# Sparse attention loop: compressed sums alternate with first scores, copies and a weight split at other places, rows turned early, first projection tiles in token halves

## What is computed

```python
def nsa_mixer(y, pos, ...):
    ...
    def block(args):                       # one block of queries
        s_c = jnp.einsum('bqghd,bngd->bghqn', qp, kc).astype(jnp.float32) * scale
        p_c = jax.nn.softmax(jnp.where(vis_c, s_c, NEG_INF), axis=-1) * vis_c
        o_c = jnp.einsum('bghqn,bngd->bqghd', p_c.astype(vc.dtype), vc)
        ...                                # top-k of blocks by p_c, keys and values k_g, v_g
        p_s = jax.nn.softmax(jnp.where(mask_s, s_s, NEG_INF), axis=-1)
        o_s = jnp.einsum('bghqm,bgqmd->bqghd', p_s.astype(v_g.dtype), v_g)
        ...
        p_w = jax.nn.softmax(jnp.where(mask_w, s_w, NEG_INF), axis=-1)
        o_w = jnp.einsum('bghqk,bkgd->bqghd', p_w.astype(vwin.dtype), vwin)
        return g[..., 0:1] * o_c + g[..., 1:2] * o_s + g[..., 2:3] * o_w
    out = lax.map(block, ...)
    return jnp.moveaxis(out, 0, 1).reshape(B, S, NSA_Q_W) @ w_out
```

## Time and profile before

| what | us |
|---|---|
| median of 3 runs (lowest, highest) | 1356.9 (1356.79, 1360.14) |
| the profiled execution, its own time | 1360.34 |
| its span | 1358.5 |
| PE busy / weight loads | 1329.3 / 1055.6 |
| DVE / ACT / POOL busy | 702.5 / 553.9 / 228.9 |
| sparse loop, first compressed sum to first WO1 matmul | 789.5 to 936.4 |

### The profile page before, as it was taken

How to read it: one execution, slowest core, us unless ns; L and a number is a source line. 1 busy time by engine, 2 the same in 40 slices (tenths; PEclk the granted TensorE clock), 3 DMA queues, 4 the chain that set the end, 5 groups by cost and what they waited for, 6 DMA issues and landing times.

```text
span 1358.5 us, 18063 instructions
## 1 busy us (share of the span) xinstructions
PE 1329.3 (98%) x6460; PEld 1055.6 (78%) x6460; DVE 702.5 (52%) x1287; ACT 553.9 (41%) x1016; POOL 228.9 (17%) x233
## 2 busy tenths in 40 slices
PE   9999999999999999999999989998999999999998
PEld 7777688888888888888877855556888888888887
DVE  4479886543343333232798667776433433342222
ACT  5435765433333332222363446775433223332221
POOL 2047571221111111001000002112211111110010
PEclk9999999999999999999999899999999999999999
DMA  7331222333333333322344200000333333333311
GB/s 240 83 77 48 62 63 78 90 88 101 93 93 98 103 110 107 102 83 78 94 124 118 75 16 1 1 17 14 96 93 93 93 96 104 93 116 107 92 57 62
DMA packets 203945, 114.12 MB, mean 84 GB/s; under 512 B 5712, under 2 KB 200528, under 8 KB 203760
## 3 DMA queue, kind: packets, MB, share of 16 engines
q1 hardware_dynamic: 203264, 112.97, 28.6%
q0 software_dynamic: 416, 0.35, 0.3%
q10 hardware_dynamic: 208, 0.06, 0.0%
HBM read 111.27 MB, written 2.10 MB: 83 GB/s over the span
## 4 chain that ended last, share of the span: by engine, by line
PE 84%; DVE 6%; ACT 4%; issue 3%; POOL 1%; DVEq 0%; POOLq 0%; ACTq 0%
PE acc L672 24%; PE acc L674 24%; PE acc L673 24%; PE acc L1215 2%; PE aux L1150 1%; PE aux L1202 1%; DVE w_low L563 1%; ACT w_high L544 1%; ACT score L1646 1%; PE acc L1150 1%; PE acc L1132 1%; PE aux L842 0%; DVE step L2096 0%; PE aux L852 0%; POOL head_rms L2444 0%
## 5 line engine op out<-in xcount | busy, mean ns | idle before, releaser
L563 DVE TENSOR_TENSOR w_low<-raw,w_high 128x1024 fp32r<-128x1024 f32 (+2 forms) x185 | 246.3, 1331 | 505.1 <-ACT w_high L544 505.0
L672 PE MATMUL acc<-y_high,w_high 128*128 128x512 f32 x992 | 391.9, 395 | 2.5 <-DVE w_low L555 2.0
L674 PE MATMUL acc<-y_high,w_low 128*128 128x512 f32 x992 | 386.6, 390 | 0.0
L673 PE MATMUL acc<-y_low,w_high 128*128 128x512 f32 x992 | 386.3, 389 | 0.0
L544 ACT ACTIVATE w_high<-raw 128x1024 fp32r<-128x1024 f32 (+2 forms) x186 | 205.7, 1106 | 316.2 <-PE acc L674 309.4
L672 PEld LDWEIGHTS acc<-y_high,w_high 128*128 128x128 f32 x992 | 185.8, 187 | 43.1 <-DVE w_low L555 3.4
L674 PEld LDWEIGHTS acc<-y_high,w_low 128*128 128x128 f32 x992 | 185.7, 187 | 40.0
L673 PEld LDWEIGHTS acc<-y_low,w_high 128*128 128x128 f32 x992 | 185.9, 187 | 38.7 <-issue 0.7
L672 PE MATMUL acc<-ffn_high,w_high 128*128 128x512 f32 (+1 forms) x374 | 141.0, 377 | 0.0
L674 PE MATMUL acc<-ffn_high,w_low 128*128 128x512 f32 (+1 forms) x374 | 140.8, 377 | 0.0
L673 PE MATMUL acc<-ffn_low,w_high 128*128 128x512 f32 (+1 forms) x374 | 140.8, 377 | 0.0
(11 more groups left out here) (335 smaller groups left out, 1707.3 us busy)
## 6 DMA issues: line engine op xcount, KB each, us to landing
raw<-in_l_w_in_dram SPq DMA_DIRECT2D x44, 512.0 KB, 3.8
raw<-in_l_w_gate_dram SPq DMA_DIRECT2D x44, 512.0 KB, 3.8
raw<-in_l_w_up_dram SPq DMA_DIRECT2D x44, 512.0 KB, 3.8
raw<-in_l_w_down_dram SPq DMA_DIRECT2D x32, 704.0 KB, 4.5
raw<-in_l_w_out_dram SPq DMA_DIRECT2D x16, 512.0 KB, 3.6
x_rows<-in_x_dram SPq DMA_DIRECT2D x4, 512.0 KB, 6.2
raw<-in_l_cmp_w_k_dram SPq DMA_DIRECT2D x4, 512.0 KB, 3.8
raw<-in_l_cmp_w_v_dram SPq DMA_DIRECT2D x4, 512.0 KB, 4.0
```

Source lines behind the costliest of these rows:

```text
L563: dve.tensor_tensor(dst, src, high.bitcast(F32), ALU.subtract).then_inc(S("split_low"), 1)
L672: pe.matmul(o, ah, bh, start=first, stop=False)
L673: pe.matmul(o, ah, bl, start=False, stop=False)
L674: return pe.matmul(o, al, bh, start=False, stop=last)
```

## The change

- Order at the loop's head: cmp_sum(0), sets 2 and 3, cmp_sum(1), sets 4 and 5, cmp_sum(2), sets 6 and 7, cmp_sum(3), takes. The last cmp_probs_T tile moves to the place of probs_T so that set 7 may overwrite its old one.
- Copies of takes: in rounds of four sets DVE's first goes behind the second maximum instead of the third. In rounds 16 to 19 ACT's go behind the fourth and seventh exponential instead of the second and fourth, DVE's behind the eighth maximum (and after it) instead of the fifth and eighth. In rounds 20 to 23 DVE has one behind the fourth maximum and ACT one behind the sixth exponential (in round 20 the second copy of each stands after all eight); where w is 1, odd takes now go to ACT. In round 1 all copies come after the exponentials and maxima.
- batch_coef goes from the start of a round to the end of the round before; coef has three places instead of two.
- The second WO1 unit's split goes from round 17 to round 12 (ACT) and 13 (DVE).
- Row groups are turned in rounds 17, 18, 19, 20 (one each, query tiles 2 and 3) and 24 (two), the last two inside WO1 as before, now through the TURN banks and in their rotation.
- The first two WO1 units are done together: tokens 256 to 511 of both, then tokens 0 to 255 of both. WO1 begins in banks 2 and 3.

```diff
@@
+        elif kind == "WO1":
+            b = (2, 3, 0, 1)[k % 4]
@@
-    return batch_tiles(TAKES[t][0] // 8) >= 2 and t % 2 == 0
+    return t % 2 == (batch_tiles(TAKES[t][0] // 8) == 1)
+
+def places_of_takes(k, act):
+    sets = sets_in(k)
+    if not sets or k == 1:
+        return ()
+    if len(sets) == 4:
+        return (0, 1) if act else (1, 3)
+    if batch_tiles(sets[0] // 8) == 1:
+        return (5,) if act else (3,)
+    return (3, 6) if act else (7,)
@@
+ROWS_AT = {17: [(2, 0)], 18: [(2, 1)], 19: [(3, 0)], 20: [(3, 1)], 24: [(1, 0), (1, 1)]}
+ROWS = [rows for _k in sorted(ROWS_AT) for rows in ROWS_AT[_k]] + [(0, 0), (0, 1)]
...
@@ PE
             cmp_sum(1)
-            cmp_sum(2)
             for k in range(1, END_ROUND):
                 for n in sets_in(k):
-                    if n == 6:
-                        cmp_sum(3)
                     set_scores(n)
+                    if n in (5, 7):
+                        cmp_sum(n // 2)
...
-                if k == len(ROUNDS):
-                    for q in range(4):
-                        rows_turn(q)
-                if k == END_ROUND - 1:
-                    for q in range(4, 6):
-                        rows_turn(q)
+                for q in rows_turned_in(k):
+                    rows_turn(q)
...
-            for first, end in ((P, T), (0, P)):
-                pe.wait_ge(S("mix_low"), MIXED + (6 if first else 8))
...
+            for first, ready in ((256, 4), (0, 8)):
+                tokens = slice(first, first + 256)
+                for m in range(2):
+                    unit_split(u + m)
+                    wait_bank(pe, ("WO1", m))
+                    pe.wait_ge(S("mix_low"), MIXED + ready)
+                    for k in range(KT):
...
@@ ACT
-                if k == 17:
+                if k == 12:
                     split_high(act, FIRST["WO1"] + 1)
...
-                behind = (0, 1) if len(sets) == 4 else (1, 3)
+                behind = places_of_takes(k, True)
@@ DVE
-                if k == 17:
+                if k == 13:
                     split_low(dve, FIRST["WO1"] + 1)
-                for b in range(BATCHES):
-                    if LAST_ROUND[b] + 2 == k:
-                        batch_coef(b)
-                behind = (2, 3) if len(sets) == 4 else (4, 7)
+                behind = places_of_takes(k, False)
...
                 for t in taken:
                     take_probs(dve, t)
+                for b in range(BATCHES):
+                    if LAST_ROUND[b] + 1 == k:
+                        batch_coef(b)
```

More of the change, by code:

```diff
@@ L300, in on_act, with rows_turned_in, last_batch @@
 def on_act(t):
-    return batch_tiles(TAKES[t][0] // 8) >= 2 and t % 2 == 0
+    return t % 2 == (batch_tiles(TAKES[t][0] // 8) == 1)
[8 more added lines that the diff above has]
+    return (3, 6) if act else (7,)
 def taken_before(t):
     return sum(on_act(k) == on_act(t) for k in range(t + 1))
+ROWS_AT = {17: [(2, 0)], 18: [(2, 1)], 19: [(3, 0)], 20: [(3, 1)], 24: [(1, 0), (1, 1)]}
+ROWS = [rows for _k in sorted(ROWS_AT) for rows in ROWS_AT[_k]] + [(0, 0), (0, 1)]
+def rows_turned_in(k):
+    return [ROWS.index(rows) for rows in ROWS_AT.get(k, ())]
+def last_batch(q):
+    i, half = ROWS[q]
+    return max(b for b in range(BATCHES) if set_of(8 * b)[0] == i and b % 2 == half)
 TURNS = []
-for _k in range(END_ROUND + 1):
-    TURNS += [("probs", t) for t in takes_in(_k - 1)] + [("sums", b) for b in ended_in(_k - 1)]
+for _k in range(END_ROUND):
+    TURNS += ([("probs", t) for t in takes_in(_k - 1)] + [("sums", b) for b in ended_in(_k - 1)]
+              + [("rows", q) for q in rows_turned_in(_k)])
+TURNS += [("sums", BATCHES - 1), ("rows", 6), ("rows", 7)]
 TURN_AT = {turn: p for p, turn in enumerate(TURNS)}
@@ L433, in trunk @@
         vhid = [row(f"v_hidden{s}", 28 + s, 1) for s in range(2)]
-        cT = [row(f"cmp_probs_T{i}", 36 + i, 1) for i in range(TT)]
+        cT = [row(f"cmp_probs_T{i}", 36 + i, 1) for i in range(TT - 1)]
+        cT.append(place(f"cmp_probs_T{TT - 1}", T, F32, y_at + 4 * 8 * T))
         hrow = row("hidden_rows", 30, 1)
@@ L1228, in rows_turn @@
             def rows_turn(q):
[L1229 to L1234, removed]
+                i, half = ROWS[q]
+                pe.wait_ge(S("o_added"), last_batch(q) + 1)
+                wait_turn_bank(("rows", q))
                 for m in range(4):
                     f = i * D + (4 * half + m) * P
-                    mm = pe.transpose(SCORE[q % 4][:, col(m)], oacc[:, f:f + P], ident)
+                    mm = pe.transpose(turn_bank(("rows", q))[:, col(m)], oacc[:, f:f + P], ident)
                 mm.then_inc(S("rows_turned"), 1)
@@ L1263, in _ @@
             u = FIRST["WO1"]
-            unit_split(u)
-            wait_bank(pe, ("WO1", 0))
-            for first, end in ((P, T), (0, P)):
-                pe.wait_ge(S("mix_low"), MIXED + (6 if first else 8))
[L1268 to L1279, removed]
+            pe.wait_ge(S("s_max"), NSETS)
+            for first, ready in ((256, 4), (0, 8)):
[5 more added lines that the diff above has]
+                    for k in range(KT):
+                        f = slice(k * T + first, k * T + first + 256)
+                        s = (u + m) % SPL
+                        mm = mm3(ps(("WO1", m))[:, tokens], wh[s][:, col(k)], wl[s][:, col(k)],
+                                 oh[:, f], ol[:, f], k == 0, k == KT - 1)
+                        if first and (m, k) == (0, 1):
+                            sums_turn(BATCHES - 1)
+                        if first and (m, k) == (0, 4):
+                            rows_turn(6)
+                        if first and (m, k) == (1, 0):
+                            rows_turn(7)
+                    if first == 0:
+                        mm.then_inc(S("unit_done"), 1)
+            for m in range(2, 8):
                 feature_unit(u + m, ("WO1", m), source=(oh, ol))
@@ L1627, in rows_high @@
             def rows_high(q):
[L1628 removed]
+                i, half = ROWS[q]
                 act.wait_ge(S("rows_turned"), q + 1)
                 act.activation(oh.rearrange("p (m t) -> p m t", t=T)[:, 4 * half:4 * half + 4, col(i)],
[L1631 removed]
+                               turn_bank(("rows", q)).rearrange("p (m t) -> p m t", t=P), ACT.Copy)\
                    .then_inc(S("mix_high"), 1)
@@ L1661, in _ @@
                     take_probs(act, t)
-                for q in range(4) if k == len(ROUNDS) else range(4, 6) if k == END_ROUND - 1 else ():
+                for q in rows_turned_in(k):
                     rows_high(q)
```

22 lines of the change are left out of this document (12 added, 10 removed).

## The result

The changed kernel takes 1363.0 us (median of 8 runs, 1361.6 to 1366.8) against 1359.3 for the kernel before (8 runs, 1356.8 to 1360.3). The ratio is 1.0029, 95% interval 1.002 to 1.0037: **some 4 us slower**, outside the range of the prediction. The profiled execution took 1362.95 us for a span of 1361.2.

The account below looks back on a forecast made before the run. PE was taken as the bound, busy 98% of the span, with time only in waits or lower clock. Terms summed to -4.1 us at full clock; one 1.7 us clock fall gave -2.4, so 1354.5 from median 1356.9, range 1348 to 1360.

Parts of the forecast that it names:

- the diff touches nothing else: Opening claim that the change reaches only the second layer's sparse loop, where the slices with less PE work lie.
- head, to round 2: Rounds 0 and 1: scores between compressed sums end the o_rows wait, 16.7 to 11.7 us, 5.0 saved.
- rounds 2 and 3: Loop rounds after the head: 9.35 us before, 1.7 of it clock; 3.0 and 5.5 us forecast, 0.85 saved.
- rounds 16 to 20: Late loop rounds: PE waits for ACT's later copies, 35.8 us before, 42.7 after, 6.9 lost.
- rounds 21 to 25: Loop's end: a copy moved from DVE to ACT and row groups gone, 22.5 to 18.7 us, 3.8 saved.
- projection to its third tile: First two projection tiles: 256-column matmuls and no o_low wait, 14.9 to 13.3 us, 1.6 saved.
- Rival (2): Later copies cost nothing; rounds 16 to 20 take PE's own 34.1 us, total 1344.2; chance 0.12.
- The split: Second output weight's split, moved to rounds 12 and 13: 0.45 us lost there; round 17 loses its 2.02 us wait.
- The clock: One fall of PE's granted clock behind round 20's 2.0 us wait, costing 1.7 us; chance of one fall 0.42.
- Rival (4): Waits of rounds 17 to 20 keep PE's clock at the lower level through half of them: 1363; chance 0.06.
- Rival (3): At the loop's head the alternation fails and PE still waits 4 us for o_rows: 1359; chance 0.06.
- Rival (1): No fall of the clock in the changed loop: 1352.8; chance 0.18.

Follow-up runs that it names:

- a1: The kernel before with one edit, the arena 128 bytes further on; 1367.8 us, ratio 1.0071 to the kernel before.
- a2: The changed kernel with coef back at 16 columns, so the arena begins where it did before; 1353.9 us, ratio 0.9965 to the kernel before.
- b1: The changed kernel without its arena shift, copies of rounds 16 to 19 behind the same sets as before; 1350.4 us, ratio 0.9933 to the kernel before.
- b3: The changed kernel without its arena shift, second output weight's split back in round 17; 1355.5 us, ratio 0.9972 to the kernel before.
- c1: The kernel before with 128 bytes free ahead of the raw and split weights and the arena 256 bytes further on; 1380.2 us, ratio 1.0153.
- d1: The kernel before with 32 bytes free ahead of the weights and the arena 64 bytes further on; 1383.4 us, ratio 1.0175.
- a4: The kernel before with the arena 64 bytes further on; 1361.7 us, ratio 1.0025 to the kernel before.
- c2: The kernel before with 32 bytes free ahead of y_high and the arena 192 bytes further on; 1368.3 us, ratio 1.0067.
- c3: The kernel before with 128 bytes free ahead of y_high and the arena 224 bytes further on; 1367.3 us, ratio 1.0059.
- b2: The changed kernel without its arena shift, compressed sums 2 and 3 back in their old places; 1363.7 us, ratio 1.0048 to the kernel before.

## Why the prediction was wrong, point by point

**The step that failed** is a clause in the first paragraph: "the diff touches nothing else". It was read as a statement on instructions, and for these it is true. `place("coef", 24)` had no term in the sum; it moves every operand in the arena by 128 bytes, and costs 9.1 us (a1) or 9.2 (a2) in the medians, 8.9 or 7.4 at equal clock. In the medians the sign of the result comes from this alone. Without the shift the change takes 1353.9 (a2; with a shift of 256 bytes, a3, 1355.3), against a forecast of 1354.5. That they meet is in good part luck: the forecast was 2.4 us off a median of 1356.9, the kernel before took 1358.7 beside a2, and at equal clock the gain that was forecast isn't there at all (last point of this section).

The terms, as the prediction gave them, and as the trace after has them:

| term | forecast us | trace after |
|---|---|---|
| head, to round 2 | 11.7 | 11.8 |
| rounds 2 and 3 | 8.5 | 8.7 |
| rounds 4 to 15, with the split | +0.25 | -0.1 |
| rounds 16 to 20 | 42.7 | 43.5 |
| rounds 21 to 25 | 18.7 | 18.8 |
| projection to its third tile | 13.3 | 12.9 |
| sum against before | -4.1 | -3.6 |

- **Rounds 16 to 20** were right in mechanism and place: two waits of 0.9 us in each of rounds 17 to 19, one of 1.94 in round 20. b1 confirms that the copies cause them. Rival (2), that they cost nothing, falls.
- **The split** was right in cost (0.35 against 0.45) and wrong in gain. The prediction counted the 2.02 us wait of round 17 as the split's; b3 shows that the later copies hold PE there for 0.95 of it anyway, so moving the split gave 0.1 to 0.4 us and not two.
- **The clock.** One fall in the loop was counted; the profile after has none, not even behind the wait of 1.94. Rival (4) names 1363, the time that came out, but its mechanism isn't there: the clock is 1.00 through rounds 17 to 20. Here are two of these stretches in the kernel after:

```profile
890.00:900.00 10.00, 8.15 (x56) 4.93 (x54) 5.17 (x22) 6.20 (x20) 0.91 (x1) 1.00 0.01 3
900.00:910.00 10.00, 8.15 (x54) 4.64 (x50) 6.43 (x23) 6.20 (x20) 1.63 (x2) 1.00 0.00 0
```

- **What the sum compared.** The -4.1 was called "at full clock", but the times before that it was taken against hold two stretches at the lower clock, 3.4 us. Part of the first stretch also lies in the head's 16.7 us, though the prediction puts all of its 1.7 into rounds 2 and 3. At equal clock the loop is 158.4 before and 158.2 to 158.5 after. By stages the kernel after stands to the one before as follows: to round 4 3.8 us less, rounds 4 to 15 0.1 less, rounds 16 to 20 9.4 more (43.5 against 34.1), rounds 21 to 25 3.7 less, the projection 2.0 less. Of the 9.4, the copies of rounds 16 to 19 make 5.5 (b1); the rest holds the row groups that moved here and the wait of 1.94 us in round 20. The gain of a2 over the kernel before, 4.8 us in the medians, comes with fewer such stretches (mean clock 0.997 to 0.999 in its six runs, 0.992 to 0.996 in 19 runs of the kernel before), not with less work or waiting in total. a3, in effect the same kernel, had 0.994 to 0.999 in twelve runs and gained 3.4 us. Whether the change brings the fewer stretches isn't shown.

Rival (3) falls with the first row of the table. Rival (1), no fall, was priced at 1352.8; the profile of a2, with none in the loop, took 1353.8.

## What to carry to other kernels

A tile that grows by a few bytes moves everything placed behind it: list the start addresses of PE's operands before and after a change, and for matmuls like these keep moving operand and weights at the same remainder by 256 bytes, the best of the distances tried. When a trace of before holds stretches at the lower clock, take them out of it ahead of comparing it with a sum at the full clock, and count them apart. A bundle of edits is worth splitting: here one of the parts took back what the others gave, and one head edit alone beat the whole.

## What the hardware showed that was not expected

- The spacing of back-to-back 512-column fp32r matmuls depends on where the moving operand lies to the weights: 0.227 us at a distance of 0 by 256 bytes, 0.229 at 64, 0.233 to 0.234 at 32, 96, 128, 160 and 224. If all 512-column stages are off, as in c1 and d1, the kernel takes 20 to 25 us more. PE reads as fully busy in all cases; only the count in a stretch, or the spacing of starts, tells.
- Stretches at the lower clock come in pieces that cost 1.7 us each. All seven profiles with the head of before (before, a1, a4, c1, c2, c3, d1) have one between 800 and 830 us, none of the ten with the new order or without copies in round 1 does. b2, which still waits 1.82 and 1.53 us for o_rows, has none there either, so in that execution the waits didn't bring it; but it is the fastest of b2's six runs, and four others had a mean clock of 0.992 to 0.993 with no trace kept. Each kernel has one profile, and what brings the stretches isn't settled by these runs.
